# A tuned decoder layer on one core: the RMS norms ahead of both networks inverted as 128x4 numbers and spread over the partitions through DRAM

## What is computed

```python
def rms_norm(x, g):
    x32 = x.astype(jnp.float32)
    y = x32 * lax.rsqrt(jnp.mean(x32 * x32, axis=-1, keepdims=True) + EPS)
    return (y * g.astype(jnp.float32)).astype(x.dtype)

def swiglu(x, w_gate, w_up, w_down):
    return (jax.nn.silu(x @ w_gate) * (x @ w_up)) @ w_down

    h = x + 0.5 * swiglu(rms_norm(x, ffn1_norm), ffn1_w_gate, ffn1_w_up, ffn1_w_down)
    ...
    h = h + 0.5 * swiglu(rms_norm(h, ffn2_norm), ffn2_w_gate, ffn2_w_up, ffn2_w_down)
    return rms_norm(h, final_norm)
```

## Time and profile before

| | |
|---|---|
| median of three runs | 2040.35 us (2038.75 to 2042.17) |
| the profiled execution, its own time | 2041.41 us |
| its span in the trace | 2039.6 us |
| PE busy | 2012.3 us, 99% |
| PEld busy | 1639.7 us, 80% |
| DVE busy | 1361.8 us, 67% |
| ACT busy | 783.8 us, 38% |
| POOL busy | 83.2 us, 4% |
| chain that ended last | PE 94%, DVE 3%, issue 1%, ACT 1% |

### The profile page before, as it was taken

One profiled execution on the slowest core, in us unless ns is written; L12 is line 12 of the kernel. 1 busy time (PEld: TensorE's weight loads), 2 busy tenths in 40 slices (PEclk: granted clock), 3 DMA queues, 4 the chain that ended last, 5 costly groups with the idle time before them and its releaser, 6 DMA issues.

```text
span 2039.6 us, 26315 instructions
## 1 busy us (share of the span) xinstructions
PE 2012.3 (99%) x9358; PEld 1639.7 (80%) x9358; DVE 1361.8 (67%) x2329; ACT 783.8 (38%) x1479; POOL 83.2 (4%) x94
## 2 busy tenths in 40 slices
PE   8999999999999999999999999999999999999998
PEld 6878888888888777777777888888888888888886
DVE  7986666666988454555676443458876666666976
ACT  6343333334455243333454112135433323334453
POOL 1000000000022000100100000000000000000021
PEclk9999999999999999999999999999999999999998
DMA  5233343257444211111114111114233223267433
GB/s 186 78 121 125 117 134 111 87 178 276 160 126 153 99 42 42 33 32 43 44 61 146 61 51 42 52 42 150 103 104 109 104 98 109 92 219 248 139 103 119
DMA packets 97563, 221.23 MB, mean 108 GB/s; under 512 B 20159, under 2 KB 20195, under 8 KB 95648
## 3 DMA queue, kind: packets, MB, share of 16 engines
q1 hardware_dynamic: 69568, 164.66, 24.1%
q10 hardware_dynamic: 22800, 46.29, 6.6%
q0 software_dynamic: 5072, 8.68, 1.3%
HBM read 164.41 MB, written 59.08 MB: 110 GB/s over the span
## 4 chain that ended last, share of the span: by engine, by line
PE 94%; DVE 3%; issue 1%; ACT 1%; DMA 0%; DVEq 0%; ACTq 0%; POOLq 0%; POOL 0%; SPq 0%
PE bank L1982 20%; PE bank L1984 20%; PE bank L1983 20%; PE bank L1926 10%; PE bank L1928 10%; PE bank L1927 10%; PE bank L2132 2%; PE bank L2169 2%; PE bank L2145 1%; DVE op_l L1382 0%; DVE B_l L1376 0%; DVE gs_l L1416 0%; PE bank L2182 0%; PE bank L1950 0%; DMA h<-xT 0%
## 5 line engine op out<-in xcount | busy, mean ns | idle before, releaser
L1926 PE MATMUL bank<-xh,wh 128*128 128x512 f32 x640 | 256.0, 400 | 0.0
L1982 PE MATMUL bank<-B_h,op_h 128*128 128x512 f32 x624 | 245.6, 394 | 8.7 <-DVE op_l L1382 8.4
L1982 PE MATMUL bank<-T_h,op_h 128*128 128x512 f32 x640 | 249.3, 390 | 1.9 <-DVE U L1473 1.9
L1927 PE MATMUL bank<-xl,wh 128*128 128x512 f32 x640 | 250.1, 391 | 0.0
L1928 PE MATMUL bank<-xh,wl 128*128 128x512 f32 x640 | 250.1, 391 | 0.0
L1983 PE MATMUL bank<-T_l,op_h 128*128 128x512 f32 x640 | 249.0, 389 | 0.0
L1984 PE MATMUL bank<-T_h,op_l 128*128 128x512 f32 x640 | 249.0, 389 | 0.0
L1984 PE MATMUL bank<-B_h,op_l 128*128 128x512 f32 x624 | 243.6, 390 | 0.0
L1983 PE MATMUL bank<-B_l,op_h 128*128 128x512 f32 x624 | 243.5, 390 | 0.0
L1982 PE MATMUL bank<-gs_h,op_h 128*128 128x512 f32 x616 | 240.5, 390 | 0.7 <-DVE gs_l L1416 0.7
L1984 PE MATMUL bank<-gs_h,op_l 128*128 128x512 f32 x616 | 239.7, 389 | 0.0
(11 more groups left out here) (208 smaller groups left out, 3380.9 us busy)
## 6 DMA issues: line engine op xcount, KB each, us to landing
gr<-g_ops SPq DMA_DIRECT2D x154, 256.0 KB, 2.7
raw<-stream SPq DMA_DIRECT2D x56, 512.0 KB, 3.5
gate<-ffn_in SPq DMA_DIRECT2D x44, 512.0 KB, 4.0
up<-ffn_in SPq DMA_DIRECT2D x44, 512.0 KB, 4.9
g_ops<-tT SPq DMA_DIRECT2D x78, 256.0 KB, 2.0
g_ops<-gb SPq DMA_DIRECT2D x58, 256.0 KB, 5.1
A<-ffn_down ACTq DMA_DIRECT2D x6, 1536.0 KB, 7.3
h_spill<-h ACTq DMA_DIRECT2D x32, 256.0 KB, 2.8
```

Of the source, the lines that this page charges most:

```text
L1926: nc.tensor.matmul(out, wh[slot][:, cols], hi, start=first, stop=False)
L1927: nc.tensor.matmul(out, wh[slot][:, cols], lo, start=False, stop=False)
L1982: nc.tensor.matmul(out, op_h[slot][:, cols], hi, start=first, stop=False, skip_group_check=True)
```

## The change

The sums of norms 0 and 2 are made with the operands the other way round: `acc[hf]` is the weight operand, read with a step of 4 tokens, and one column of `ones` moves, so that four matmuls (each of one column) leave token 4p+c in partition p, column c of the bank. ACT takes the root of 128x4 numbers into the new tile `rstd_4`, DVE inverts 128x4. POOL stores these 2 KB to the new DRAM tensor `rstd_tok`, waits for the store, and loads the 512 numbers back into all 128 partitions of `rstd`. All readers of `rstd` in the networks wait for that load (`rstd_in`) where they waited for the inversion (`rstd_done`). ACT takes the first half's root between the squares of the second half, and DVE inverts it between the second half's additions. In network 1 the first sum is made ahead of step 6 where it was ahead of step 7.

```diff
-SUM_AT = ((5, 8), (7, 9))
-INVERT_AT = ((6, 9), (7, 9))
+SUM_AT = ((5, 8), (6, 9))
+INVERT_AT = (9, 9)
...
+    rstd_4 = place("rstd_4", [P, 4], at(218))
...
+            def lay_out_rstd(f, hf):
+
+                n = 2 * f + hf
+                pool.wait_ge(rstd_4_made, n + 1)
+                pool.dma_start(rstd_tok[n].rearrange("(p c) -> p c", c=4), rstd_4[:]).then_inc(rstd_out, 16)
+                pool.wait_ge(rstd_out, 16 * (n + 1))
+                pool.dma_start(rstd[:, hf * HALF:(hf + 1) * HALF], rstd_tok[n].partition_broadcast(P)).then_inc(rstd_in, 16)
...
                 pool.dma_start(bias_rows[first:first + n, :], rows[0:n, v, :]).then_inc(rows_out, 16)
+            lay_out_rstd(0, 0)
             pool.wait_ge(rows_out, 64)
+            lay_out_rstd(0, 1)
...
             for hf in range(2):
+                lay_out_rstd(1, hf)
+            for hf in range(2):
                 add_squares(3, hf)
...
                 act.wait_ge(ssq, 2 * norm + hf + 1)
+                if norm % 2 == 0:
+                    if norm + hf:
+                        act.wait_ge(rstd_out, 16 * (norm + hf))
+                    nc.scalar.activation(rstd_4[:], bank[NORM_BANK[norm][hf]][:, 0:4], ACT.Sqrt, bias=eps[:, 0:1]).then_inc(root, 1)
+                    return
...
-                    if j in SUM_AT[f]:
-                        root_of(2 * f, SUM_AT[f].index(j))
+                    if j == SUM_AT[f][1]:
+                        root_of(2 * f, 1)
...
                 square(0, 1, n)
+                if n == 3:
+                    root_of(0, 0)
...
                 square(2, d // 8, d % 8)
+                if d == 12:
+                    root_of(2, 0)
...
+            def invert_4(norm, hf):
+
+                dve.wait_ge(root, 2 * norm + hf + 1)
+                nc.vector.reciprocal(rstd_4[:], rstd_4[:]).then_inc(rstd_4_made, 1)
...
                 for k in range(1, KT):
+                    if hf and k == 6:
+                        invert_4(norm, 0)
...
-                dve.wait_ge(rstd_done, 4 * f + hf + 1)
+                dve.wait_ge(rstd_in, 16 * (2 * f + hf + 1))
...
-                    if j in INVERT_AT[f]:
-                        invert(2 * f, INVERT_AT[f].index(j))
+                    if j == INVERT_AT[f]:
+                        invert_4(2 * f, 1)
...
                 pe.wait_ge(sq_sum, adds_before(norm, hf) + KT - 1)
+                if norm % 2 == 0:
+                    tokens = acc[hf][:].rearrange("p (t c) -> p c t", c=4)
+                    for c in range(4):
+                        last = nc.tensor.matmul(bank[NORM_BANK[norm][hf]][:, c:c + 1], tokens[:, c], ones[:, 0:1], start=c == 0, stop=True,
+                                                skip_group_check=True)
+                    last.then_inc(ssq, 1)
+                    return
```

More of the change, by code:

```diff
@@ L332, with build @@
 RESULT_ORDER = [(0, k) for k in range(KT)] + [(1, k) for k in (4, 5, 6, 2, 7, 3, 0, 1)]
-def build(nc, xT, ffn_in, ffn_down, stream, gains, b_in, sinks, rel_bias, onehot, bias_rows, bias_rep, h_spill, g_ops, gz, stat_tok, outT):
+def build(nc, xT, ffn_in, ffn_down, stream, gains, b_in, sinks, rel_bias, onehot, bias_rows, bias_rep, h_spill, g_ops, gz, stat_tok, rstd_tok, outT):
     f32, f32r = mybir.dt.float32, mybir.dt.float32r
@@ L514, in build @@
         rstd_done = sem("rstd_done")
+        rstd_4_made = sem("rstd_4_made")
+        rstd_out = sem("rstd_out")
+        rstd_in = sem("rstd_in")
         x_high = sem("x_high")
@@ L1323, in invert @@
                 invert_part(norm, hf, 0, 1)
-                dve.wait_ge(rstd_done, 2 * norm + hf + 1)
+                dve.wait_ge(rstd_done, norm - 1 + hf + 1)
+            def invert_4(norm, hf):
+                dve.wait_ge(root, 2 * norm + hf + 1)
+                nc.vector.reciprocal(rstd_4[:], rstd_4[:]).then_inc(rstd_4_made, 1)
             def add_squares(norm, hf):
                 for k in range(1, KT):
+                    if hf and k == 6:
+                        invert_4(norm, 0)
                     dve.wait_ge(sq_done, 16 * norm + 8 * hf + k + 1)
@@ L1583, in result @@
                 if hf == 0:
-                    dve.wait_ge(rstd_done, 7)
+                    dve.wait_ge(rstd_done, 3)
                 nc.vector.scalar_tensor_tensor(out=hg[:, k, cols], in0=h[:, k, cols], scalar=gain[:, 3, k:k + 1],
@@ L2298 @@
     bias_rows = nc.dram_tensor("bias_rows", (HEADS, VEC), mybir.dt.float32, kind="Internal").ap()
+    rstd_tok = nc.dram_tensor("rstd_tok", (4, HALF), mybir.dt.float32, kind="Internal").ap()
     bias_rep = nc.dram_tensor("bias_rep", (HEADS, P, VEC), mybir.dt.float32, kind="Internal").ap()
@@ L2304 @@
     outT = nc.dram_tensor("outT", (D_MODEL, SEQ), mybir.dt.float32, kind="ExternalOutput").ap()
-    build(nc, *args, bias_rows, bias_rep, h_spill, g_ops, gz, stat_tok, outT)
+    build(nc, *args, bias_rows, bias_rep, h_spill, g_ops, gz, stat_tok, rstd_tok, outT)
     r = run_bass_kernel_spmd(nc, [arrays], core_ids=[0])
```

## The result

The changed kernel takes 2045.08 us in the median of 11 runs (2043.8 to 2047.98), the kernel before 2040.81 us beside it. The ratio is 1.0021, with a 95% interval of 1.0013 to 1.0029. So it is slower by about 4.3 us, 2.7 to 5.9, and lies above the range that was given. The profiled execution took 2043.8 us, with a span of 2042.0.

The account below looks back on a forecast made before the run. PE was taken as the bound, busy 99%. DVE 0, ACT 0, trips 0 and PE's sums +0.4 on 2040.35 made 2040.8 us, no measurable change (89%); range 2038.0 to 2043.4.

Parts of the forecast that it names:

- The sums: On PE, four one-column matmuls replace each sum of 0.91 us: about 0.9 us, taken as +0.1 each, +0.4 us in all.
- The upper bound: For PE's stepped weight reads: 1.66 times, from ACT's reordering copies, giving +0.53 us for each sum, +2.1 in all.
- The rival of the stepped loads: PE's stepped weight loads are slow: at 1.66 times +2.1 us, 2042.5; chance 15%, of which 4% beyond 0.2%.
- the doubling that was worked out beside the Trainium skill's rule: If the 16-byte-line rule doubled each PE weight load, the four sums would add 3.2 us and give 2043.6.
- The inversions at nothing: DVE's four inversions shrink to 128x4, freeing 12.6 us, costed at nothing because DVE is tied to PE's pace.
- the `U2` waits: PE's waits for `U2` at tile 4, one per network, 1.9 us together, were to stay; rival that they go: 7%.
- the freed time at 95 us: DVE, already idle 1.88 us at 95.19 before an `op_l`, would only wait longer there.
- The roots: On ACT, table load and root between the squares delay the fifth by about 1.2 us; PE's second sum keeps 0.6.
- The trips: POOL's store and load of `rstd` through DRAM: 5.2 us each, covered by PE's plain steps; late-trip rival 4%.
- The deadline of 10.6 us: Latest `rstd` for PE's step 12 in network 0: 44.7, 10.6 us after the inversion at 34.1.
- The hold-up of POOL's DMAs by DVE: DVE's use of the shared port could add 2.5 us per DMA, a trip of about 10 us, the sum the same.
- The clock: Rival: one-column matmuls at each PE sum lower the clock, +3.0 us a sum, 2052.6; chance 3%.

## Why the prediction was wrong

- **The sums (the step that failed).** "I take +0.1 for each, +0.4 us, near the row of the same instruction." Measured: 1.79 in place of 0.91, +0.88 for each, +3.5 us in all. The row of the same instruction had weights side by side, and the whole price lies in the step, which no row showed. The upper bound, a factor of 1.66 from ACT's copies, was no bound: the factor is 2.05 (1.66 over 0.81 us). The rival of the stepped loads, with 15%, was the case that came, at the doubling that was worked out beside the Trainium skill's rule (+3.2 us, 2043.6, just outside the range that ended at 2043.4). With that term the sum would have given 2040.35 + 3.5 = 2043.9, and the range should have reached to the case of doubled loads. The measured difference is 4.3 us, 2.7 to 5.9; the 0.8 us above 3.5 lie inside the interval.
- **The inversions at nothing: right, for a reason that holds earlier than was said.** DVE lost 13.3 us, the `U2` waits stayed 1.9 us, and the kernel without inversions took the same time. But the prediction looked for the freed time at 95 us; most of it was already idle time by 53.40.
- **The roots: right for PE.** ACT's load and root stand between the squares, the second sum is not waited for, and in network 1 ACT waits 0.9 us for the first sum (PE reaches it at 1397.55, not 1395.80, late by the two sums of network 0). The inversion there starts at 1402.14 and not at 1400.0, which delays the trip but not PE.
- **The trips: covered, but mis-sized.** 6.3 and 7.9 us in place of 5.2, since the load took 4.1 us in the median and not the 3.0 of `z_in`. `t` started 1.1 us sooner in network 0 and 4.3 us later in network 1 (1.4 us later with unstepped weights, where PE is on time). The second half's trip was not wholly covered in network 1 either: `t` waited 0.54 us for it at 1422.27. The deadline of 10.6 us that was computed from step 12 was not the only one: in network 1 the second half has another at tile 4, through DVE's backlog, and it was missed by 2.0 us when each trip was 3.0 to 3.8 us longer. That no such wait came in the changed kernel was in part luck, since this deadline was not in the working.
- **The hold-up of POOL's DMAs by DVE, from the Trainium skill (SBUF — State Buffer, "SBUF: two separate sides")**, is not seen here. The 4.1 us of the load are more than `z_in` took, but a load issued at 40.48 in the run with one more load, while DVE was idle (36.9 to 44.00), also took 3.5 us, and one at 51.16, beside a DVE that was busy for 2.1 us of it, no more than 3.7. These rows speak against DVE as the cause; what makes the load longer stays open.
- **The clock: right for this kernel**, 1.00 around the sums. The bursts of 1.66 us didn't lower it. The rival was nearer than its 3%: two bursts in a row, 2.56 us, did lower it.

## What to carry to other kernels

When the bound engine is given a new access pattern, its price has to be found before anything else is counted; a row of the same instruction with another pattern bounds it from one side only. A weight operand of fp32 could here be read with a step of 2 numbers for nothing, while a step of 4 doubled the time of the burst. And on a chain that reaches the bound engine only through slack, follow every reader of the late value, not only the first wait: here the second half's normalised operands came due before the bank that looked tightest. And DVE's idle time in front of a late load costs nothing only as long as a later gap makes up for it; behind the second half's load there are 46.6 us without one.

None of the versions beats the kernel before by an amount that can be measured; the step of 2 gives back what the change lost and no more.

## What the runs showed of the hardware

- Four one-column fp32 matmuls with 128x128 weights hold up PE 0.81 us at a step of 1, 0.85 at 2, 1.25 at 3 and 1.66 at 4.
- A store of 2 KB from 128 partitions to DRAM, issued by POOL, took 2.0 to 3.1 us from one issue to the next in 128 runs of 16 bytes, 3.6 to 5.9 in 256 of 8, and 8.5 to 9.5 in 512 of 4.
- With the store in 512 runs, the granted clock was at its 1.2 GHz level for about 3 us behind each of two waits of 2.4 us in PE's stream, and for 5 us behind waits of 3.8 and 4.0; waits of 1.1 and 2.0 us (with one more load) left it at 1.00. The slow matmuls cost 8.9 us on top of 12.6 us of waits.
- The clock also fell without a wait: behind 2.56 us of one-column matmuls in a row it was at 0.50 for about 3.5 us, 1.6 us lost, while behind 1.66 us of them it stayed at 1.00.
